# Expert step in quarters with the down product between them, and the recurrence's masks ahead of the linear scan

## Time and profile before

| what | value |
|---|---|
| median of three runs | 1370.47 us |
| time of the profiled execution | 1379.81 us |
| its span, first to last instruction | 1377.6 us |
| mean granted TensorE clock | 0.905 |
| PE busy / DVE busy / ACT busy | 1136.6 / 634.6 / 288.6 us |
| DMA, mean over the span | 117 GB/s |

### The profile page before, as it was taken

How to read it: one execution, slowest core, us unless ns; L and a number is a source line. 1 busy time by engine, 2 the same in 40 slices (tenths; PEclk the granted TensorE clock), 3 DMA queues, 4 the chain that set the end, 5 groups by cost and what they waited for, 6 DMA issues and landing times.

```text
span 1377.6 us, 18600 instructions
## 1 busy us (share of the span) xinstructions
PE 1136.6 (83%) x7301; PEld 664.4 (48%) x7301; DVE 634.6 (46%) x1300; ACT 288.6 (21%) x540; POOL 143.0 (10%) x163
## 2 busy tenths in 40 slices
PE   2599988899789998899898896995467889889483
PEld 1245557766667667666577543543322223233130
DVE  3614693258732786337943379465300011111086
ACT  2214132142321432214312400111000011111211
POOL 3100200001000000001000031222000000000144
PEclk9999999899989999899997797997588999999885
DMA  9554410002100111001210412110775675756362
GB/s 342 199 181 171 140 46 1 2 20 58 31 1 1 39 39 31 1 16 31 61 80 1 190 54 87 51 51 17 290 316 220 249 276 205 274 212 216 131 229 99
DMA packets 51136, 160.54 MB, mean 117 GB/s; under 512 B 22904, under 2 KB 23112, under 8 KB 40440
## 3 DMA queue, kind: packets, MB, share of 16 engines
q1 hardware_dynamic: 40904, 126.40, 26.2%
q0 software_dynamic: 6560, 22.07, 4.6%
q10 hardware_dynamic: 3600, 11.11, 2.1%
HBM read 328.90 MB, written 22.59 MB: 255 GB/s over the span
## 4 chain that ended last, share of the span: by engine, by line
PE 57%; DVE 25%; DMA 9%; issue 3%; ACT 2%; SPq 1%; POOL 1%; ACTq 0%; POOLq 0%; DVEq 0%
PE ps L762 14%; PE ps L1062 7%; PE ps L1149 7%; PE ps L885 7%; PE ps L1164 5%; DMA arena<-in_w_gu 4%; DMA arena<-in_w_dn 3%; DVE arena L1680 3%; DVE arena L1682 3%; PE ps L988 1%; PE ps L924 1%; DVE arena L1727 1%; PE ps L728 1%; PE ps L968 1%; DMA arena<-in_b_ada 1%
## 5 line engine op out<-in xcount | busy, mean ns | idle before, releaser
L762 PE MATMUL ps<-arena 128*128 128x348 f32 (+5 forms) x1056 | 320.9, 460 | 4.6 <-DVE arena L1566 4.6
L762 PEld LDWEIGHTS ps<-arena 128*128 128x128 f32 (+2 forms) x1056 | 194.3, 187 | 126.9 <-issue 27.5
L1149 PE MATMUL ps<-arena 128*32 128x512 f32 x1280 | 152.1, 628 | 40.0 <-DMA arena<-in_w_gu 24.4
L1062 PE MATMUL ps<-arena 128*128 128x512 f32 (+1 forms) x288 | 131.3, 612 | 0.0
L1149 PEld LDWEIGHTS ps<-arena 128*32 128x32 f32 x1280 | 42.2, 115 | 136.7 <-issue 113.0
L2030 DVE TENSOR_TENSOR arena<-arena,ps 128x256 f32<-128x256 f32 x20 | 8.5, 423 | 212.5 <-ACT arena L1443 212.5
L885 PE MATMUL ps<-arena 128*128 128x128 f32 (+3 forms) x896 | 91.1, 287 | 0.7 <-ACT arena L1351 0.5
L1164 PE MATMUL ps<-arena 128*32 128x512 f32 x640 | 77.4, 626 | 13.5 <-DMA arena<-in_w_dn 13.5
L885 PEld LDWEIGHTS ps<-arena 128*128 128x128 f32 (+2 forms) x896 | 85.1, 188 | 6.8 <-issue 2.7
L1062 PEld LDWEIGHTS ps<-arena 128*128 128x128 f32 (+1 forms) x288 | 52.2, 186 | 67.7 <-issue 67.5
L900 PE MATMUL ps<-arena 64*128 64x256 f32 x256 | 47.6, 524 | 28.5 <-ACT arena L1267 22.6
(11 more groups left out here) (393 smaller groups left out, 1566.9 us busy)
## 6 DMA issues: line engine op xcount, KB each, us to landing
arena<-in_w_gu SPq DMA_DIRECT2D x160, 1024.0 KB
arena<-in_w_dn SPq DMA_DIRECT2D x80, 1024.0 KB
arena<-in_w_ada SPq DMA_DIRECT2D x24, 1024.0 KB, 5.1
arena<-in_w_in SPq DMA_DIRECT2D x20, 512.0 KB, 3.9
slot_scr<-arena ACTq DMA_DIRECT2D x20, 512.0 KB, 7.2
arena<-in_x_all SPq DMA_DIRECT2D x16, 512.0 KB, 11.1
arena<-in_w_out SPq DMA_DIRECT2D x8, 512.0 KB, 7.5
h_scr<-arena SPq DMA_DIRECT2D x8, 512.0 KB, 2.6
```

The lines of the kernel that those rows point to most:

```text
L762: mm = T.matmul(ps[0:rows, c, 0:w], lhs(k), hT[:, k, c0:c0 + w], start=(k == 0), stop=(k == KC - 1))
L1062: mm = T.matmul(ps[0:rt, 2 * (i % 2) + n, :], yT[:, k, r0:r0 + rt], wout[:, k, 512 * n:512 * n + 512], start=(k == 0), stop=(k == KC - 1))
L1149: mm = T.matmul(ps[r_, 2 + b, :], xgt[b][:, k, r_], exgu[c][:, k, :], start=(k == 0), stop=(k == KC - 1))
```

## The change

**Experts.** Gate and up are loaded in quarters of 0.5 MB per column (4096-byte rows, before 8192), with four semaphores. PE's step s becomes: quarters 0 and 1 of `gate_up(s)`; `turn_hidden(s-1)`; `turn_rows` for s+1; `down(s-1)`; quarters 2 and 3 of `gate_up(s)`. SP's order follows: quarter 0, quarter 1, down, quarter 2, quarter 3. ACT and DVE are put in the matching order. The loops over steps are written out in full.

**Mixer.** The LRU tiles move to buffers that the masks do not write: `pk`, `pr`, `tmp`/`Y`, `gbuf[9]` and one new tile. DVE's order behind the shift of v becomes: bonus, square, `q_ready`, the four masks of half 0, then the two gate steps, the multiplier, the scan and the gating. ACT's square roots move behind the gate projection's last chunk. PE's `turn` no longer waits for `prep_done`; ACT's first key chunk of the next block does.

```diff
-        ld_gu = [sem(f"ld_gu{i}") for i in range(2)]
+        ld_gu = [sem(f"ld_gu{i}") for i in range(4)]
-        lru_bufs = [gbuf[5 * n:5 * n + 5] for n in range(2)]
+        xc_late = take(HALF)
+        lru_bufs = [[(gbuf[9], xc_late)[n], pk[:, PAD + HALF * n:PAD + HALF * n + HALF], pr[:, PAD + HALF * n:PAD + HALF * n + HALF],
+                     (tmp, Y)[n], gbuf[2 + n]] for n in range(2)]
...
-                cols = slice(2048 * h, 2048 * h + 2048)
+                cols = slice(D_MODEL * h, D_MODEL * h + D_MODEL)
...
-                    for hf_ in range(2):
-                        sp.wait_ge(gu_mm, 2 * s + hf_ + 1)
-                        load_gu(hf_, ex_next, ch_next)
-                if s:
-                    sp.wait_ge(dn_mm, s)
-                    load_dn(ex, ch)
+                for q in range(4):
+                    if s < STEPS - 1:
+                        sp.wait_ge(gu_mm, 4 * s + q + 1)
+                        load_gu(q, ex_next, ch_next)
+                    if s and q == 1:
+                        sp.wait_ge(dn_mm, s)
+                        load_dn(ex, ch)
...
-                    if hf == 0:
-                        pe.wait_ge(HV["prep_done"], j + 1)
...
+            def gate_up(s, b, q):
+                pe.wait_ge(ld_gu[q], 16 * NCT * s + 16 * NCT)
+                for k in (2 * q, 2 * q + 1):
...
-            def step(s, i, b, more):
-                pe.wait_ge(xgt_out, s + 1)
-                gate_up(s, b)
-                pe.wait_ge(hidt_out, s)
...
-                down(s, 1 - b)
-                if more:
-                    pe.wait_ge(ld_xg[1 - b], 16 * i + 16 * (1 + b))
-                    turn_rows(s, 1 - b)
-                pe.wait_ge(hid_out, s + 1)
-                turn_hidden(s, b)
+            for s in range(STEPS):
+                b = s % 2
                 pe.wait_ge(xgt_out, s + 1)
+                gate_up(s, b, 0)
+                gate_up(s, b, 1)
+                if s:
+                    pe.wait_ge(hid_out, s)
+                    turn_hidden(s - 1, 1 - b)
+                if s < STEPS - 1:
+                    pe.wait_ge(ld_xg[1 - b], 16 * ((s + 1) // 2) + 16)
+                    turn_rows(s + 1, 1 - b)
+                if s:
+                    pe.wait_ge(hidt_out, s)
+                    if s > 1:
+                        pe.wait_ge(ys_out, s - 1)
+                    down(s - 1, 1 - b)
+                gate_up(s, b, 2)
+                gate_up(s, b, 3)
...
-                project_out(6 + 5 * j, None, multipliers, gate=j)
+                project_out(6 + 5 * j, None, gate=j)
+                for hf in range(2):
+                    act.wait_ge(HV["q_ready"], 2 * j + hf + 1)
+                    t2 = lru_bufs[hf][3]
+                    A.activation(t2, t2, ACT.Sqrt).then_inc(HV["lru_mult"], 1)
...
                         if g == 0 and hf and j < NJ - 1:
+                            act.wait_ge(HV["prep_done"], j + 1)
                             chunk_out(7 + 5 * j, 0, pk)
...
+            for s in range(1, STEPS):
+                b = s % 2
+                hidden_copy(s - 1, 1 - b)
+                if s < STEPS - 1:
+                    rows_copy(s + 1, 1 - b)
+                store(s - 1, 1 - b)
+                hidden(s, b)
...
-                link(shift_tile(2, pv, MU_V))
+                link(shift_tile(2, pv, MU_V, gbuf[0], gbuf[1]))
...
+                for n in range(2):
+                    o = PAD + n * HALF
+                    dve.wait_ge(HV["bonus_mm"], 2 * j + n + 1)
+                    TT(kept[n][7], ps[:, 3 + 2 * n, :], pv[:, o:o + HALF], ALU.mult).then_inc(HV["bonus_out"], 1)
                 for n, (xc, tr, ti, t2, hs) in enumerate(lru_bufs):
                     dve.wait_ge(HV["lru_exp"], 2 * j + n + 1)
                     lag(TT(hs, tr, tr, ALU.mult))
+                last_done()
+                for xc, tr, ti, t2, hs in lru_bufs:
+                    last = STT(out=t2, in0=hs, scalar=1.0, in1=t2, op0=ALU.add, op1=ALU.mult)
+                    last.then_inc(HV["q_ready"], 1)
+                dve.wait_ge(HV["q_ready"], 2 * j + 2)
+                strict_b(4 * j)
+                strict_b(4 * j + 1)
+                strict_k(4 * j)
+                strict_k(4 * j + 1)
...
+            for s in range(1, STEPS):
+                dve_ys(s - 1, 1 - s % 2)
+                dve_hid(s, s % 2)
+            dve_ys(STEPS - 1, 1)
```

More of the change, by code:

```diff
@@ L1141, in turn_rows @@
                 mm.then_inc(xg_turned, 1)
[L1143 to L1151, removed]
+            def gate_up(s, b, q):
+                pe.wait_ge(ld_gu[q], 16 * NCT * s + 16 * NCT)
+                for k in (2 * q, 2 * q + 1):
+                    for c in range(NCT):
+                        r_ = slice(COLT * c, COLT * c + COLT)
+                        mm = T.matmul(ps[r_, 2 + b, :], xgt[b][:, k, r_], exgu[c][:, k, :], start=(k == 0),
+                                      stop=(k == KC - 1))
+                mm.then_inc(gu_mm, 1)
             def turn_hidden(s, b):
@@ L1170, in _ @@
             turn_rows(0, 0)
[L1171 to L1176, removed]
-            def step(s, i, b, more):
-                pe.wait_ge(xgt_out, s + 1)
-                gate_up(s, b)
-                pe.wait_ge(hidt_out, s)
-                if not (isinstance(s, int) and s == 1):
-                    pe.wait_ge(ys_out, s - 1)
-                down(s, 1 - b)
-                if more:
-                    pe.wait_ge(ld_xg[1 - b], 16 * i + 16 * (1 + b))
-                    turn_rows(s, 1 - b)
-                pe.wait_ge(hid_out, s + 1)
-                turn_hidden(s, b)
[L1192 to L1197, removed]
+            for s in range(STEPS):
+                b = s % 2
+                pe.wait_ge(xgt_out, s + 1)
+                gate_up(s, b, 0)
[13 more added lines that the diff above has]
+                gate_up(s, b, 3)
+            pe.wait_ge(hid_out, STEPS)
+            turn_hidden(STEPS - 1, 1)
             pe.wait_ge(hidt_out, STEPS)
             pe.wait_ge(ys_out, STEPS - 1)
-            down(STEPS, 1)
+            down(STEPS - 1, 1)
             for i, (r0, rt) in enumerate(TILES):
@@ L1450, in store @@
                 act.wait_ge(ys_out, s + 1)
-                act.dma_start(slot_scr.rearrange("(s p) d -> s p d", p=P)[bass.ds(s, 1)].rearrange("s p d -> (s p) d"),
+                act.dma_start(slot_scr[P * s:P * s + P, :],
                               ys[:, b, :]).then_inc(slot_stored[b], 16)
             rows_copy(0, 0)
+            rows_copy(1, 1)
             hidden(0, 0)
-            rows_copy(1, 1)
-            hidden_copy(0, 0)
-            def act_step(s, b, more):
-                hidden(s, b)
[L1461 to L1471, removed]
+            for s in range(1, STEPS):
[4 more added lines that the diff above has]
+                store(s - 1, 1 - b)
+                hidden(s, b)
+            hidden_copy(STEPS - 1, 1)
             store(STEPS - 1, 1)
@@ L1713, in _ @@
                     y_ = yT[:, NJ + j, HALF * n:HALF * n + HALF]
-                    last = TT(y_, hs, y_, ALU.mult)
+                    last = TT(y_, ti, y_, ALU.mult)
                 done(last, HV["prep_done"], j + 1)
```

98 lines of the change are left out of this document (36 added, 62 removed).

## The result

| | before | after |
|---|---|---|
| median of the runs, us | 1373.18 (1369.93 to 1380.44, 4 runs) | 1334.51 (1332.44 to 1338.51, 4 runs) |
| ratio, 95% interval | | **0.9722** [0.9694, 0.9751] |
| profiled execution, us (span) | 1379.81 (1377.6) | 1336.12 (1334.0) |
| first expert row transposes start, us | 991.2 | 963.9 |
| expert stage: from there to the end of the last down product, us | 306.3 | 289.5 |

The change is faster by 38.7 us, where 64 were forecast. The range ended at 1330, so the time is outside it.

A forecast was written before the change was run, and what follows sets the result against it. The chain of waits was taken as PE 57%, DVE 25%, DMA 9%. Mixer 23.6 us and experts 40.3 us, together 64, put the profiled execution at 1315.9 and the median, 9.3 lower, at 1306 us; range 1294 to 1330.

The forecast's parts named there:

- The mixer part: Four mixer blocks: masks and Gram products come earlier, saving 5.9 us a block, 23.6 us in all.
- The steady step: Undisturbed expert step: PE's 0.97 us wait for the row copy goes, step 11.75 us, 18.4 us saved over 19.
- rival 2: Expert step: the wait moves to the turned hidden rows, 0.97 us a step, +18 us, 1324; chance 0.07.
- the tail: End of expert stage: two quarters cover half the last down weights' wait; last down product ends 7.0 us later.
- rival 3: Expert steps: written-out code streaming in stalls each step behind queued loads, slower at 1401 us; chance 0.04.
- The step that failed: Gate and up loads after step 1: two columns' quarters take 2.5 us in about 10, so waits go.
- down weights: Down loads in the expert stage: PE waits 8 us in all, with 3.4 us of slow clock behind two.
- step 1: Start of the second expert step: begins 1.3 us earlier because a quarter lands sooner, still runs 2.1 us slow.
- Rival 1: Expert loads: weights keep the pace, gate waits of 11.7 us stay, +20 us, 1326; chance 0.16.
- The conversion to a median: Whole kernel: the median lies 9.3 us below the profiled execution, so 1315.9 there becomes 1306.

The follow-up runs named there:

- mixer_only: Kernel before with only the mixer part of the change, expert stage as before: 1352.46 us, ratio 0.9861 to before.
- halves: Changed kernel with gate and up weights loaded in two 1 MB halves again, PE's new order kept: 1342.52 us, ratio 0.9803 to before.
- static_q: Changed kernel with quarters, expert numbers fixed in the program, SP issuing only loads that move data, no register reads: 1311.3 us, ratio 0.9559 to before.
- lean: Changed kernel without SP's change-flag reads; a load's condition is the difference of two expert numbers: 1340.18 us, ratio 0.9725 to before.
- static_h: Changed kernel with expert numbers fixed in the program, only loads that move data, gate and up in halves: 1315.49 us, ratio 0.9568 to before.
- early_act: Changed kernel with SP's register reads one step ahead, and down loads with eight reads of their own on ACT's queue: 1316.9 us, ratio 0.9600 to before.

## Why the prediction was wrong, point by point

**The mixer part** held: 6.1 us a block by the trace against 5.9, by the rows that were named. mixer_only has 19.1 us in time (13.5 to 24.9) where 23.6 stood; the interval holds it.

**The steady step** held: 11.68 against 11.75, no wait for the turned hidden rows in it (rival 2 is out), and the tail is 6.85 (the last gate product ends at 1246.58, the last down product at 1253.43) against 7.0. An undisturbed step has no gap in which code could have been waited for, and the whole is faster, so rival 3 is out.

**The step that failed** is this sentence on gate and up: "a quarter becomes free every 1.7 us or behind the down product, and each has about 10 us [...] I take these waits as gone." The 10 us were right (9.8). What was set against them was 2.5 us, the bytes of two columns at full rate, as if a load were asked for the moment its buffer is free and had the queues to itself. Both halves of that failed.

- *The issue* was priced at nothing. The prediction's own 1.7 us is the time between the release of quarter 3 and that of the next step's quarter 0. In it SP has four conditional loads (1.4 us if they move nothing) and eight register reads (4.4): an estimate from these rows is 5.8 less 1.7, 4.1 us late, and quarters 0 and 1 were issued 4.6 us late on average, up to 7.2 behind a change of two columns. In the old order the same reads had some 9 us between the second half's release and the next first half's, and the lag was 1.70. So it was PE's new order that laid the reads bare, even with halves (2.58), and eight more conditional loads a step made SP's sum 11.4 us in a step of 11.7.
- *The transfer* took 5.9 to 7.6 us from the issue to the landing, not 2.5. That is measured; the reason is argued only: the other quarters, the down weights, rows and stores are on the way at the same time.

Either alone would have fitted into 9.8 us: static_q has transfers of 6.2 to 7.6 and waits of 1.8 us, and a lag of 4.6 with 2.5 us behind it would be 7.1 (an estimate, no run shows it). Together they were 10.4 us for quarter 0 and 11.6 for quarter 1. Measured: 12.6 us of waits, and some 6 of matrix products that ran slow behind them. The longest of these, and its window (us, busy by engine, PEclk, DMA share, GB/s):

```profile
1154.10 6.59 PE L1149 MATMUL ps<-arena 128*32 128x512 f32 x32 [3.47 <-DMA arena<-in_w_gu]
...
1154.10:1160.70 6.60, 6.57 (x33) 1.34 (x34) 0.00 (x0) 0.00 (x0) 0.00 (x0) 0.57 1.01 418
```

Half of the undisturbed 64 is 3.5 us; the granted clock was 0.57 here, and the queues ran full. Two more such rows make up the 6. Waits and slow products are 18.6 of the 23.5 us by which the stage missed its forecast; step 1 began 2.1 late (24.3 after the first transposes, 22.2 forecast), and down weights make up the rest (10.5 us of waits before the tail, where 8 stood).

**Rival 1** had the size (gate waits stay, 11.7) for a reason that is half right at best. A transfer lasts 5 to 9 us by the means of all kernels, well over its bytes at the full rate, which fits loads that share the queues, and waits for down weights stay even in static_q (9.6 us). But volume does not hold up gate and up by itself: static_q has the same bytes in time, and smaller loads did not take longer from issue to landing than larger ones. The Trainium skill, "DMA: Bandwidth & Descriptors", section "Bandwidth", asks for at least 1 MiB a load, by measurements of loads that GpSimd issues; with fixed addresses 0.5 MB and 1 MB, issued by SP, gave stages of 268.0 and 268.1 us, so no run here shows a loss for loads of this size. The fit that the prediction took with it (2.0 us plus bytes over 436 GB/s) stands in that page's section "Anatomy of one DMA — SWDGE (gpsimd) path", for the same kind of loads; its estimate of 3.2 us for a quarter compares with 5.9 to 7.6 measured in after, with other loads on the way. What the smaller size cost here is the number of loads the queue's engine must issue.

**The conversion to a median** was wrong too: the profiled execution before lay 9.3 us above the median, and the forecast carried that over. After, it lies 1.6 above. The trace forecast was 1315.9 for the profiled execution, which took 1336.12: 20.2 of the 28.5 us of error are the kernel, the other 8 are this. Kernels with the old mixer began the expert stage at 984.3 and 986.3 in other profiles, not 991.2, so by these two that excess lay in front of the stage and belongs to that one execution; its cause is open.

The size of the range was wrong by the same omission: a cost priced at nothing had no upper bound in it. The trace of before would have given it: SP's reads and skipped loads stand there with the same durations (a read 266 and 147 ns, a skipped load 133, 29 and 73 ns), its first half was already issued 1.7 us late, and its transfers took 6.6 to 8.4 us, not the 2.5 to 5 of bytes over the full rate.

## What to carry to other kernels

Give each engine that issues loads its own sum for a step, skipped loads and register reads included, and lay it against the moments at which buffers come free: what counts is what stands in its order between a release and the issue, not its idle time over the step. Take the transfer's time from issue to landing out of the trace, not from bytes over rate, and lay both together against the window. A wait named after a DMA can be a wait for its issue; the time from the buffer's release to the issue tells. Read registers a step ahead, in a gap in which no buffer comes free, before cutting loads into smaller ones; and let an idle engine's queue take some of them.

## What the runs showed of the hardware

- On SP a register read costs 0.55 us, a conditional load with a run-time address 0.35 us even if it moves nothing, 0.62 if it moves data (its DMA instruction is 73 ns against about 343). A condition that is a difference of two registers costs 0.06 more per load, 0.33 in the loads that work it out (lean).
- With constant addresses and no condition a load is issued 0.13 to 0.15 us after the release on average (static_q, static_h).
- The same register work on ACT's queue (a read every 0.53 us there) delayed none of its activations enough to be seen: early_act's undisturbed step is 11.7 us, as without it.
- A column's gate and up weights in two loads of 1 MB or in four of 0.5 MB, issued at once, took 7.1 to 7.6 us against 6.2 to 7.6 on average from issue to landing, and the stages were equal (268.1 and 268.0), with gate waits after step 1 of 6.4 and 1.8 us.
- A granted clock of 0.57 stood over the products behind a wait of 3.47 us (1154.10 of after): 32 took 6.59 us, where half of an undisturbed row of 64 is 3.5.
